# Couples of k-tiles, smaller first pieces, seven warm-ups, ten matmuls at the end and a last block in halves in a hybrid attention and pooling layer

## What is computed

```python
h = jnp.einsum('bsd,de->bse', x, w_in)
q, k, v, z_attn, u_pool, z_pool, g_pre = jnp.split(h, idx, axis=-1)
...
y_attn = o.astype(x.dtype) * jax.nn.silu(z_attn)
y_pool = causal_pool_mixer(u_pool, w_pool, pool_scale) * jax.nn.silu(z_pool)
...
merged = g_attn * jnp.einsum('bsc,cd->bsd', y_attn, w_proj_attn) \
    + g_pool * jnp.einsum('bsc,cd->bsd', y_pool, w_proj_pool)
out = jnp.einsum('bsd,de->bse', merged, w_out)
return layer_norm(DEEPNORM_ALPHA * x + out, ln_gamma, ln_beta)
```

## Time and profile before

| what | us |
|---|---|
| median of 3 runs | 943.73 |
| lowest and highest | 943.44, 943.92 |
| the profiled execution's own time | 944.02 |
| span of its profile, first to last instruction | 942.2 |

### The profile page before, as it was taken

One profiled execution on the slowest core, in us unless ns is written; L12 is line 12 of the kernel. 1 busy time (PEld: TensorE's weight loads), 2 busy tenths in 40 slices (PEclk: granted clock), 3 DMA queues, 4 the chain that ended last, 5 costly groups with the idle time before them and its releaser, 6 DMA issues.

```text
span 942.2 us, 14833 instructions
## 1 busy us (share of the span) xinstructions
PE 933.1 (99%) x5374; PEld 835.9 (89%) x5374; DVE 635.7 (67%) x1002; ACT 420.6 (45%) x584; POOL 0.2 (0%) x4
## 2 busy tenths in 40 slices
PE   9999999999999999999999999999999999999996
PEld 7998998998998998998998999888888888888886
DVE  7767567567567567567567567666666666666866
ACT  6454354354354354354354354545445444444340
POOL 0000000000000000000000000000000000000000
PEclk9999999999999999999999999999999999999998
DMA  9745544544544544544545546655545555557432
GB/s 377 246 167 179 191 167 179 190 166 178 189 168 178 186 170 178 187 169 178 185 171 179 185 174 223 223 182 209 189 178 188 183 209 178 187 199 284 178 134 90
DMA packets 26397, 178.30 MB, mean 189 GB/s; under 512 B 3327, under 2 KB 3583, under 8 KB 5759
## 3 DMA queue, kind: packets, MB, share of 16 engines
q1 hardware_dynamic: 25920, 173.72, 51.0%
q10 hardware_dynamic: 452, 4.24, 1.1%
HBM read 175.85 MB, written 2.10 MB: 189 GB/s over the span
## 4 chain that ended last, share of the span: by engine, by line
PE 99%; DVE 0%; issue 0%; DVEq 0%; ACT 0%
PE proj_ps L351 40%; PE proj_ps L355 20%; PE attn_ps L351 7%; PE attn_ps L343 4%; PE attn_ps L344 4%; PE attn_ps L345 4%; PE attn_ps L355 4%; PE value_ps L345 3%; PE value_ps L343 3%; PE value_ps L344 3%; PE mixed_ps L344 1%; PE mixed_ps L343 1%; PE mixed_ps L345 1%; PE mixed_ps L475 1%; PE attn_ps L412 1%; PE mixed_ps L484 0%
## 5 line engine op out<-in xcount | busy, mean ns | idle before, releaser
L351 PE MATMUL proj_ps<-xt,w_hi 128*128 128x512 f32 x1632 | 568.8, 392 | 0.0
L355 PE MATMUL proj_ps<-xt,w_lo 128*128 128x256 f32 x1632 | 455.9, 279 | 0.0
L765 DVE TENSOR_TENSOR w_lo<-w_raw,w_hi 128x1024 fp32r<-128x1024 f32 x314 | 369.2, 1220 | 70.9 <-ACT w_hi L611 69.3
L351 PEld LDWEIGHTS proj_ps<-xt,w_hi 128*128 128x128 f32 x1632 | 305.6, 187 | 68.7 <-DVE xt L787 0.4
L611 ACT ACTIVATE w_hi<-w_raw 128x1024 fp32r<-128x1024 f32 x314 | 314.1, 1051 | 42.8 <-PE mixed_ps L345 25.1
L355 PEld LDWEIGHTS proj_ps<-xt,w_lo 128*128 128x128 f32 x1632 | 308.0, 189 | 0.0
L631 ACT ACTIVATE corr<-proj_ps 128x256 f32<-128x256 f32 x102 | 39.3, 385 | 281.1 <-PE proj_ps L355 281.1
L779 DVE TENSOR_TENSOR qk_f<-proj_ps,corr 128x256 f32<-128x256 f32 x46 | 19.5, 424 | 76.6 <-ACT corr L631 76.6
L351 PE MATMUL attn_ps<-yp,w_hi 128*128 128x512 f32 x128 | 45.1, 391 | 0.0
L351 PE MATMUL attn_ps<-ya,w_hi 128*128 128x512 f32 x128 | 45.1, 391 | 0.0
L345 PE MATMUL value_ps<-w_hi,xt 128*128 128x384 f32 x128 | 42.9, 335 | 0.0
(11 more groups left out here) (168 smaller groups left out, 930.4 us busy)
## 6 DMA issues: line engine op xcount, KB each, us to landing
w_raw<-in_weights SPq DMA_DIRECT2D x158, 1024.0 KB, 4.8
first_raw<-in_first SPq DMA_DIRECT2D x8, 640.0 KB, 8.1
res<-in_x_rows ACTq DMA_DIRECT2D x1, 2048.0 KB
out_rows<-res SPq DMA_DIRECT2D x8, 256.0 KB, 2.5
gamma<-in_gamma_row ACTq DMA_DIRECT2D x1, 1024.0 KB
beta<-in_beta_row ACTq DMA_DIRECT2D x1, 1024.0 KB
mask<-in_mask SPq DMA_DIRECT2D x1, 512.0 KB, 17.9
ident<-in_identity SPq DMA_DIRECT2D x1, 64.0 KB, 17.6
```

Of the source, the lines that this page charges most:

```text
L351: mm(bank, w_hi[:, slot, k * P:(k + 1) * P], tile.rearrange("p a s -> p (a s)"), start=first, stop=False)
L355: done = mm(bank[:, SEQ:2 * SEQ], w_lo[:, slot, k * P:(k + 1) * P], tile[:, 0, :], start=False, stop=last)
L765: tt(w_lo[:, slot, cols], w_raw[:, slot, cols], w_hi[:, slot, cols].bitcast(F32), ALU.subtract).then_inc(lo_split, 1)
```

## The change

It has six parts. The first two k-tiles become pieces of their own (`SINGLE`), so that there are 9 pieces in place of 8, the first two of 320 KB; for both of them the weights of each chunk are split by themselves. `SIDE_BY_SIDE` is 6, which is again ten k-tiles. `first_part` now issues the high matmuls of all k-tiles of a piece and then the low ones, with a wait of its own for each. Seven warm-ups are issued in place of ten. Ten matmuls of 128x512 (`KEEP_UP`) stand behind the last products, ahead of the turn of the shift; nothing reads their result. The last block of tile 1 is normalised and stored in two halves of 256 columns.

```diff
-WARM_UP = 10
-
-PIECES = tuple((k, k + 2) for k in range(0, KT, 2))
+WARM_UP = 7
+KEEP_UP = 10
+
+SINGLE = 2
+PIECES = tuple((k, k + 1) for k in range(SINGLE)) + tuple((k, k + 2) for k in range(SINGLE, KT, 2))
 ABREAST = RING
-SIDE_BY_SIDE = 5
+SIDE_BY_SIDE = 6
...
+LAST_PARTS = tuple(slice(c, c + BLOCK // 2) for c in range(D_MODEL - BLOCK, D_MODEL, BLOCK // 2))
...
-            return [slice(n, n + 1) for n in range(ABREAST)] if q == 0 else [slice(0, ABREAST)]
+            return [slice(n, n + 1) for n in range(ABREAST)] if q < SINGLE else [slice(0, ABREAST)]
 
         def parts_done(n, q):
-            return n + 1 if q == 0 else ABREAST + q
+            return q * ABREAST + n + 1 if q < SINGLE else SINGLE * ABREAST + q - SINGLE + 1
...
-            for n in range(TT * BLOCKS):
+            stores = [(n // BLOCKS, slice(n % BLOCKS * BLOCK, (n % BLOCKS + 1) * BLOCK))
+                      for n in range(TT * BLOCKS - 1)]
+            stores += [(TT - 1, cols) for cols in LAST_PARTS]
+            for n, (t, cols) in enumerate(stores):
...
             def first_part(n, q):
 
+                bank, ks = first_bank(n), range(*PIECES[q])
+                pe.wait_ge(piece_hi_done, parts_done(n, q))
                 pe.wait_ge(x_lo_done, q + 1)
+                for k in ks:
+                    mm(bank, w_hi[:, n, k * P:(k + 1) * P], xt[:, k, :, :].rearrange("p a s -> p (a s)"),
+                       start=(k == 0), stop=False)
                 pe.wait_ge(piece_lo_done, parts_done(n, q))
-                for k in range(*PIECES[q]):
-                    done = k_tiles(n, (k,), lambda k: (first_bank(n), xt[:, k, :, :], k == 0, k == KT - 1))
+                for k in ks:
+                    done = mm(bank[:, SEQ:2 * SEQ], w_lo[:, n, k * P:(k + 1) * P], xt[:, k, 0, :],
+                              start=False, stop=(k == KT - 1))
                 return done
...
+            for _ in range(KEEP_UP):
+                mm(value_ps[:, :], merged[:, 0, 0, P:SEQ], last_hi[:, 0:BLOCK], start=True, stop=True)
             pe.wait_ge(shift_ready, 1)
...
-                at = res[:, t, c * BLOCK:(c + 1) * BLOCK]
-                stt(out=at, in0=at, scalar=rstd[:, 2 + t:3 + t], in1=norm_shift(c)[:, :],
-                    op0=ALU.mult, op1=ALU.add).then_inc(out_ready, 1)
+                for cols in (slice(c * BLOCK, (c + 1) * BLOCK),) if c < BLOCKS - 1 else LAST_PARTS:
+                    at = res[:, t, cols]
+                    stt(out=at, in0=at, scalar=rstd[:, 2 + t:3 + t],
+                        in1=norm_shift(c)[:, cols.start - c * BLOCK:cols.stop - c * BLOCK],
+                        op0=ALU.mult, op1=ALU.add).then_inc(out_ready, 1)
```

More of the change, by code:

```diff
@@ L323, in _ @@
                 load(n % RING, n)
-            for n in range(TT * BLOCKS):
+            stores = [(n // BLOCKS, slice(n % BLOCKS * BLOCK, (n % BLOCKS + 1) * BLOCK))
+                      for n in range(TT * BLOCKS - 1)]
+            stores += [(TT - 1, cols) for cols in LAST_PARTS]
+            for n, (t, cols) in enumerate(stores):
                 sp.wait_ge(out_ready, n + 1)
-                t, cols = n // BLOCKS, slice(n % BLOCKS * BLOCK, (n % BLOCKS + 1) * BLOCK)
                 sp.dma_start(out_d[t, :, cols], res[:, t, cols]).then_inc(out_landed, 16)
-            sp.wait_ge(out_landed, 16 * TT * BLOCKS)
+            sp.wait_ge(out_landed, 16 * len(stores))
         @block.tensor
@@ L789, in _ @@
                 for n in parts_of(q):
-                    dve.wait_ge(piece_hi_done, parts_done(n.stop - 1 if q == 0 else 0, q))
+                    dve.wait_ge(piece_hi_done, parts_done(n.stop - 1 if q < SINGLE else 0, q))
                     tt(w_lo[:, n, piece_cols(q)], piece_w(q)[:, n, :],
```

## The result

| | median us | lowest, highest | executions |
|---|---|---|---|
| before | 943.66 | 943.05, 944.06 | 12 |
| changed | 945.58 | 943.47, 947.31 | 12 |

The ratio is 1.0019, interval 1.0011 to 1.0027: slower by 1.9 us where 0.9 faster was forecast, and outside the range. The spread is as telling as the median: 1.0 us before, 3.8 us now. A constant cost would have moved the group; this one has drawn it apart, so something at the start or the end goes well in some executions and badly in others. The profiled execution is one of the bad ones, 946.73 us with a span of 944.9.

What follows compares the result with a forecast made beforehand. TensorE, busy 933.1 of 942.2 us, was taken as the bound. Gains of 0.50 (start), 0.05 (order) and 0.35 (end), 0.9 off 943.73, gave 942.83, stated as 942.9; own bounds 942.4 to 943.2, eight-in-ten range 942.4 to 943.6.

Steps and rivals of the forecast that it cites:

- First pieces: At the start: piece 0 lands near 3.55 in place of 4.32, real matmuls run from 4.95, 1.3 us earlier.
- Same bytes ahead of it, same landing: Piece of k-tiles 2 and 3 lands as the old piece 1 did, high parts there at 7.38, low weights at 8.39.
- the harm of smaller DMAs: At the first pieces: more descriptors of half the length; if they delay the last landing by 0.1, 0.1 is lost.
- The clock rival: At the start: piece 0 lands at 4.32 after all, TensorE idles, clock rises later; 944.3 us, chance 0.07.
- D/2: Cost of a delay D of the clock's rise at the start, since matmuls then run at half rate; 1.7 for D 3.35.
- Seven warm-ups: At the start: seven end at 4.95, and TensorE goes to real work without a gap.
- The lead of two high matmuls: At the first pieces: high pair goes ahead of the low weights, capped again at the last piece; 0.50 us gained, bounds 0.0 to 0.65.
- the 0.05 that I gave to the new order itself: In the 12 couples behind the cap: high matmuls before low ones gain 0 to 0.19 us, taken as 0.05.
- The end: Ten matmuls hold the clock, 0.3 us, and the last block in halves 0.05: 0.35 gained, bounds -0.15 to 0.6.
- The term for the halves: Last block in two halves of 256 columns, last store with half the bytes: 0.05 us gained, bounds -0.15 and 0.3.

Runs made afterwards that it cites:

- the short rows in one DMA: Kernel before with k-tiles 0 and 1 in two buffer halves, fetched by one 640 KB DMA with 2560-byte rows: 944.24 us against 943.84.
- ten warm-ups: The changed kernel with ten warm-ups in place of seven: 945.67 us, ratio 1.0021.
- the version that keeps it: Kernel before with high matmuls first and ten matmuls at the end, ten warm-ups kept: 943.29 us against 943.84, then 943.09 against 943.77.

## Why the prediction was wrong

- **First pieces.** The small piece came 0.57 us earlier (0.77 forecast), real matmuls started at 4.98 (4.95), at half rate (0.64 us a couple, 0.67 forecast), and the clock rose at 6.98 (about 6.35). Right, with the clock 0.6 us late, which lies within its scatter (below). On what fills the slow phase, "TensorE: Matmul & The Clock Gate" of the Trainium skill, part 1, held: the real products from 4.98 on counted as well as zeros, for the rise came at 6.98 with them and at 10.6 where TensorE idled from the seventh warm-up to 6.03.
- **"Same bytes ahead of it, same landing"** is the step that failed. The third piece came at 8.56 in place of 6.03, the last at 18.04 in place of 16.02. It was 2.0 to 2.9 us late in six of eight profiles with two DMAs for the first 640 KB and in none of nine with one. I had put the harm of smaller DMAs at 0.1 us, thinking of their row length; row length alone was worth at most 0.6 us at the first pieces and nothing at the last, as the short rows in one DMA show, and no row of before could bound the rest. By the closing packets, what came late was one engine (ten warm-ups) or six of the sixteen (changed kernel), and the last piece was still 1.5 to 2.4 us late in all six.
- **The clock rival** was named, but with the wrong trigger and 0.07. What cost the clock was not a late first piece but the late third one: TensorE had done k-tiles 0 and 1 by 8.1, idled until 10.06, and the clock fell afterwards. The price, D/2, was of the right size: 3.4 us at half rate, 1.7 us. That it equals the 1.7 of the rival is chance, since the D there was that of a late rise.
- **Seven warm-ups** were costed at nothing since the small piece would be there. With small pieces that held. By themselves, ahead of a piece of 640 KB, they lose 1.6 us in 8 of 11 executions, and with the new order and end in 6 of 11.
- **The lead of two high matmuls**, capped at both ends at 0.50 us, was of the right size in the medians: 0.55 and 0.68 us in the time of the version that keeps it, of which the ten matmuls at the end may have up to 0.2 (943.66 against 943.89 by themselves). In single executions it isn't capped at 0.50 but goes with the clock's rise: at chunk 3 it was 0.71, 0.55, 0.29 (the changed kernel with its piece in time) and 0.04 us, with the rise at 4.96, 4.68, 6.71 and 7.38. No run separates the 0.05 that I gave to the new order itself. It is the only part of the change for which the times speak: with it, together with the ten matmuls at the end, both sets lie 0.55 us or more below before.
- **The end.** The clock held and block 1 came 0.32 us earlier after block 0, as forecast (0.3). The term for the halves was mis-sized, +0.05 forecast and -0.35 measured: a half took DVE 476 ns (0.42 forecast, from other operations of 256 columns), and SP's issues of the halves 437 to 457 ns (0.33), the last of them 0.2 us later from the shift than the whole block's issue; and it landed 2.9 to 3.0 us after its issue, the whole block 2.8. PSUM is not what makes the half dear: the row sum over 256 columns reads PSUM too and takes 421 ns (L1015), and over 512 columns the same normalisation takes 751 ns from SBUF (L1049) and 742 from PSUM. That half-size transfers fare worse is also the direction of the rule of sizes in the Trainium skill, "DMA: Bandwidth & Descriptors" (Bandwidth), which I had weighed less than the rows. That the profiled execution of before had the clock fall early (7.1 us from the shift, 6.8 in seven of the eight other profiles with the old end) was an accident that I took for its rule.
- **The range.** The bounds that I gave to the terms, 0.0 to 0.65 and -0.15 to 0.6, add up to 942.5 to 943.9, not to 942.4 to 943.2. The measured 945.58 lies outside both, so the slip is not what made it wrong.

What stays open is why two smaller DMAs at the head of the queue hold up single engines some microseconds into the program, and only in most executions. One of SP's issues goes with it: in the six late profiles the longest issue of a piece took 1.0 to 1.7 us, in the two that were in time 0.53 and 0.68, and in those with one DMA of 640 KB at most 0.64 (0.94 with short rows). Whether that is cause or effect no run here tells.

## What to carry to other kernels

Being early is worth only what the next data allows, and idling ahead of it can cost the clock: order the work so that TensorE does what is ready (both high matmuls ahead of the low ones) rather than start sooner and idle. Let warm-ups reach to the first real product. Cut the pieces at the head of a DMA queue smaller only with a measurement of the landings behind them, in several profiles. When the spread of a kernel's times grows, read the profile's own time first, and take a second profile before you trust either.

## What the runs showed that I had not expected

- Two DMAs of half size ahead of large ones put the next piece 2.0 to 2.9 us late in six of eight profiles; the same small DMAs behind the large ones did nothing. The mean rate need not show it: 230 to 323 GB/s for three microseconds in one such profile, 392 to 399 in another, with one engine of sixteen 2.3 us behind the others.
- With the same ten warm-ups from 1.83 us the clock rose anywhere from 4.96 to 7.98 us, in the twelve profiles in which TensorE was busy up to the rise. Some of the spread within one kernel will come from there.
- An idle stretch of TensorE of 0.8 us ahead of the first real matmul left two groups of times 1.6 us apart in the same kernel, three executions low and eight high: it matters whether the clock has risen before the idle stretch.
- DVE needed 476 ns to normalise 256 columns of the last block, against 742 for 512: two halves cost 0.13 us more than the whole at the very end, where nothing hides it.
